# More chunks of the up stages in wide products, and a shorter lead of VectorE's subtractions, in a five-layer transformer on one core

## The chip, the core and the metric

The kernel runs on one core of one Trainium2 chip. What counts is the device time of one execution in microseconds (us), shown as the median of several runs. Engines go by their usual names: TensorE (PE in the profile; PEld is its weight load), VectorE (DVE), ScalarE (ACT), GpSimd (POOL) and SyncE (SP), which issues the weight transfers.

## What is computed

Five transformer layers on one sequence of 256 tokens and 1,024 features, all in float32: four of a first block (attention, then a gated feed-forward part), and one of a second. The feed-forward part of the first four layers is where the change lies:

```python
def conv_gated_ffn(h, w_up, conv_w, conv_b, w_down):
    u = h @ w_up
    C = u.shape[-1]
    u = lax.conv_general_dilated(u, conv_w[:, None, :].astype(u.dtype), window_strides=(1,),
                                 padding=[(CONV_W - 1, 0)], dimension_numbers=('NWC', 'WIO', 'NWC'),
                                 feature_group_count=C) + conv_b
    gate, val = jnp.split(u, 2, axis=-1)
    return (jax.nn.silu(gate) * val) @ w_down
```

`w_up` is 1,024 x 5,504 (gate and value, 2,752 features each), `w_down` 2,752 x 1,024, and the convolution takes three taps along the sequence.

## The kernel before

**Products in two parts.** A float32 matrix product is made of reduced-precision ones: every operand is kept as a high part (`w_hi`, `h_hi`) and a low part (`w_lo`, `h_lo`), and high x high, high x low and low x high are summed. `product` (line 1772 on) issues three matmuls of 256 columns for each 128 x 128 tile of weights (lines 1779 to 1781). `wide_product` (line 1785 on) issues two: the low weights with the high activations, 256 columns (line 1791), and the high weights with high and low activations side by side in `h_both`, 512 columns (line 1794). It leaves two halves in one PSUM bank, which must be added afterwards.

**Weights.** They come as 241 chunks of 1 MB. For each chunk SP issues the transfer to `w_raw` (three buffers, `RAW`), ScalarE casts it to `w_hi` (line 409), VectorE subtracts and has `w_lo` (line 953); `w_hi` and `w_lo` have five slots (`SLOTS`). SP starts the transfer of chunk c when VectorE has subtracted chunk c - 3:

```python
                if c >= RAW:
                    sp.wait_ge(lo_ready, c - RAW + 1)
```

**The up stage** has 22 chunks in a layer. Each holds 128 gate and 128 value features, which go to the banks `pj[slot]` and `val_bank[slot]`, with three slots used in turn (`RING`); chunk 21 is half of one. TensorE's first three chunks are mixed with the wait for the normalised activations (`first_outputs`, lines 1842 and 1851); then come chunks 3 to 20 one after the other, either with `outputs` (three products a tile) or `wide_outputs`, as `is_wide` says. Before each, TensorE waits for the low weights of the chunk (`lo_ready`) and for the bank to be free (`bank_free`), in `chunk_ready`.

In step j ScalarE works on chunk j in this order: for a wide chunk it copies the second halves out of the banks (line 872); it multiplies by a tap and adds the bias (line 887, twice; for a wide chunk these read the sums that VectorE makes); then it casts weight chunks up to j + `high_up(j)`, which is 4 at first and 5 from j = 3 on; then it applies the gate function (line 891). VectorE in step j: for a wide chunk it adds the halves (line 1532, twice); it adds the other taps (line 1540, four times); then it subtracts weight chunks up to j + `low_up(j)`; then, when the gate function is done, it multiplies gate and value (line 1560). GpSimd then splits the product into a high and a low part (lines 1751 and 1754). `low_up` before:

```python
            return min(AHEAD - 1, RING + j // 4)
```

that is 3 for j = 0 to 3 and 4 from j = 4 on, so step 4 subtracts two chunks.

**The down stage** follows at once. Its 11 weight chunks hold 16 tiles of 128 x 128 each in a row, 22 for each output tile. Its first product takes hidden tiles 0 to 18 of the first output tile, and waits at its start for all the weights that these need:

```python
                        n, at = divmod(f * FT + k, UNITS)
```

```python
                        pe.wait_ge(lo_ready, first + (f * FT + b - 1) // UNITS + 1)
```

With f = 0, b = 19 and `UNITS` = 16 this is the second of the down stage's weight chunks, number 23 when the up stage's are counted from 0. The second product (f = 1) needs number 24, the third output tile number 26. The last tiles (19 to 21) are taken in after both first products, when GpSimd has split the last hidden tile.

The order of work on every engine is as written: engines meet through semaphores alone.

Of the kernel before, what the change touches and what calls it, by code (L numbers as in the profile page):

```python
# [37 lines left out]
FT = 22  # L38
RING = 3
# [30 lines left out]
AHEAD = 5  # L70
HIGH = 4
RAW = 3
WIDE_UP = (range(10, 20),) * 4 + (range(2, FT),)
UNITS = STD // P
DOWN = FT * DT // UNITS

# [23 lines left out]
def build(nc, xT, w_std, params, consts, lam, onehot, tables, pT, out):  # L100
    ctx = ExitStack()
    with ctx:
# [178 lines left out]
        def is_wide(ffn, j):  # L281

            return j in WIDE_UP[ffn]

        def wide_count(ffn, j):

            return sum(len(WIDE_UP[f]) for f in range(ffn)) + j - WIDE_UP[ffn][0] + 1

# [41 lines left out]

        def low_up(j):

            return min(AHEAD - 1, RING + j // 4)

        def down_weights(c0, k):

# [604 lines left out]
        def _(dve):  # L941
# [291 lines left out]
            for kind, c0, n in STAGES:  # L1233
# [244 lines left out]
                elif kind == "up":  # L1478
                    def half_step(j, c, slot):
                        at = j * 8 + PARAM["conv"] + ffn * FT * 8  # L1480
                        dve.wait_ge(conv_init, (j + ffn * FT) * 2 + 2)
                        dve.scalar_tensor_tensor(cgate[:, slot, 1:S], pj[slot][:, 0:S - 1], par[:, at + 1:at + 2],
                                                 cgate[:, slot, 1:S], ALU.mult, ALU.add).then_inc(conv_part, 3)
                        dve.wait_ge(conv_part, (j + ffn * FT) * 3 + 3)
                        dve.scalar_tensor_tensor(cgate[:, slot, 2:S], pj[slot][:, 0:S - 2], par[:, at:at + 1],
                                                 cgate[:, slot, 2:S], ALU.mult, ALU.add).then_inc(bank_free, 1)
                        split_to(weights_of(layer, c) + low_up(j))
                        dve.wait_ge(gated, j + ffn * FT + 1)
                        dve.tensor_tensor(cval[0:HALF, slot, :], cgate[0:HALF, slot, :], cval[0:HALF, slot, :],
                                          ALU.mult).then_inc(prod_done, 1)  # L1490
# [82 lines left out]
                    for j in range(n):  # L1573
                        step(j, c0 + j, slot_of(c0, j), lambda: split_to(weights_of(layer, c0 + j) + low_up(j)))
# [999 lines left out]
```

## Time and profile before

| | us |
|---|---|
| median of 3 runs | 1479.22 |
| lowest, highest | 1477.85, 1479.90 |
| the profiled execution | 1477.22 |
| its span, first to last instruction | 1475.6 |
| TensorE busy in it | 1469.5 (100%) |
| VectorE busy | 1114.9 (76%) |
| ScalarE busy | 922.8 (63%) |
| GpSimd busy | 331.5 (22%) |
| weight load on TensorE, beside its matmuls | 1366.6 (93%) |
| DMA, mean rate | 180 GB/s |

The profile shows one execution. Busy times are sums over the span and say nothing of who waits for whom; that is read from the chain that ended last, and from the instructions of two engines laid side by side in time. Matmuls overlap in the pipeline, so the time that one costs is the distance between two starts and not the duration in its row.

### The profile page before, as it was taken

Reading aid. Unit: us, or ns where it says so; the run is one execution under the profiler, and the core shown is the slowest. Engines: PE = TensorE matmul, PEld = TensorE weight load, DVE = VectorE, ACT = ScalarE, POOL = GpSimd, SP = SyncE. Lnnn points to the kernel's source line nnn. Section 1 sums busy time; section 2 is a strip of 40 time slices with the busy share of each in tenths; the row PEclk is TensorE's granted clock in tenths of the full one; section 3 lists DMA queues with packets and bytes.
Section 4 is the critical chain, followed back from the end, with each engine's and each line's share of the span. In section 5 each row is a group of like instructions: output and inputs, shape, how many; then the busy total and the mean of one; then the engine's idle time right before and its main releaser. Section 6 shows DMA issues by size and latency. Waiting matters only on the chain.

```text
span 1475.6 us, 26859 instructions
## 1 busy us (share of the span) xinstructions
PE 1469.5 (100%) x10616; PEld 1366.6 (93%) x10616; DVE 1114.9 (76%) x1877; ACT 922.8 (63%) x1528; POOL 331.5 (22%) x461
## 2 busy tenths in 40 slices
PE   9999999999999999999999999999999999999999
PEld 8999989899999898989989899999898999988998
DVE  7778898565578995787899566688995688798645
ACT  7776666456766664575676456766764558566443
POOL 2104222211142222212222221022212361122100
PEclk9999999999999999999999999999999999999999
DMA  7644656444346555562565545445655464366450
GB/s 276 203 159 138 223 199 222 169 162 161 115 138 208 201 203 194 184 189 87 200 208 196 196 161 197 157 142 202 209 192 199 157 215 171 115 213 209 176 209 30
DMA packets 39689, 265.06 MB, mean 180 GB/s; under 512 B 5247, under 2 KB 5562, under 8 KB 8976
## 3 DMA queue, kind: packets, MB, share of 16 engines
q1 hardware_dynamic: 36432, 255.54, 49.1%
q0 software_dynamic: 2992, 7.79, 2.2%
q8 instruction: 84, 1.38, 0.4%
q14 instruction: 37, 0.30, 0.1%
q10 hardware_dynamic: 144, 0.05, 0.0%
HBM read 262.24 MB, written 1.12 MB: 178 GB/s over the span
## 4 chain that ended last, share of the span: by engine, by line
PE 98%; ACT 1%; DVE 1%; DMA 1%; issue 0%; SPq 0%; ACTq 0%
PE bank L1794 26%; PE bank L1779 15%; PE bank L1780 14%; PE bank L1781 14%; PE bank L1791 13%; PE bank L1842 6%; PE bank L1851 3%; PE bank L2025 1%; PE bank L2014 1%; PE bank L2006 1%; PE bank L2005 1%; PE bank L2379 1%; PE bank L2026 1%; DMA w_raw<-w_std 1%; PE bank L2078 0%; PE bank L2193 0%
## 5 line engine op out<-in xcount | busy, mean ns | idle before, releaser
L953 DVE TENSOR_TENSOR w_lo<-w_raw,w_hi 128x2048 fp32r<-128x2048 f32 x239 | 549.8, 2308 | 72.5 <-ACT w_hi L409 72.4
L409 ACT CAST w_hi<-w_raw 128x2048 fp32r<-128x2048 f32 x239 | 453.3, 1905 | 82.2 <-DMA w_raw<-w_std 61.9
L1794 PE MATMUL bank<-h_both,w_hi 128*128 128x512 f32 x960 | 301.5, 395 | 0.0
L1779 PE MATMUL bank<-h_both,w_hi 128*128 128x256 f32 x992 | 284.6, 287 | 0.0
L1780 PE MATMUL bank<-h_both,w_hi 128*128 128x256 f32 x992 | 280.6, 283 | 0.0
L1781 PE MATMUL bank<-h_both,w_lo 128*128 128x256 f32 x992 | 280.5, 283 | 0.0
L1791 PEld LDWEIGHTS bank<-h_both,w_lo 128*128 128x128 f32 x960 | 180.0, 188 | 42.2
L1794 PE MATMUL bank<-act_both,w_hi 128*128 128x512 f32 x672 | 212.0, 395 | 0.0
L1779 PEld LDWEIGHTS bank<-h_both,w_hi 128*128 128x128 f32 x992 | 189.9, 191 | 5.0 <-issue 4.2
L1780 PEld LDWEIGHTS bank<-h_both,w_hi 128*128 128x128 f32 x992 | 190.0, 192 | 0.3
L1781 PEld LDWEIGHTS bank<-h_both,w_lo 128*128 128x128 f32 x992 | 189.9, 191 | 0.0
L1791 PE MATMUL bank<-h_both,w_lo 128*128 128x256 f32 x960 | 188.6, 278 | 0.0
L1751 POOL CAST act_both<-tmp 128x256 f32 x110 | 53.9, 490 | 438.1 <-DVE tmp L1560 319.1
L1779 PE MATMUL bank<-act_both,w_hi 128*128 128x256 f32 x516 | 149.2, 289 | 0.0
L1791 PEld LDWEIGHTS bank<-act_both,w_lo 128*128 128x128 f32 x672 | 124.1, 188 | 26.6
L1794 PEld LDWEIGHTS bank<-h_both,w_hi 128*128 128x128 f32 x960 | 146.1, 189 | 0.0
L1780 PE MATMUL bank<-act_both,w_hi 128*128 128x256 f32 x516 | 145.9, 283 | 0.0
L1781 PE MATMUL bank<-act_both,w_lo 128*128 128x256 f32 x516 | 145.9, 283 | 0.0
L1791 PE MATMUL bank<-act_both,w_lo 128*128 128x256 f32 x672 | 135.2, 279 | 0.0
L1540 DVE SCALAR_TENSOR_TENSOR tmp<-u_sb,par,tmp 128x255 f32<-128x255 f32 x234 | 113.2, 524 | 21.7 <-ACT tmp L887 20.9
L1842 PE MATMUL bank<-h_both,w_hi 128*128 128x256 f32 x400 | 106.7, 288 | 0.3 <-DVE w_lo L1139 0.2
L1794 PEld LDWEIGHTS bank<-act_both,w_hi 128*128 128x128 f32 x672 | 103.7, 189 | 1.5
(233 smaller groups left out, 2651.1 us busy)
## 6 DMA issues: line engine op xcount, KB each, us to landing
w_raw<-w_std SPq DMA_DIRECT2D x239, 1024.0 KB, 4.9
act_both<-vec_dram POOLq DMA_DIRECT2D x56, 128.0 KB, 3.5
w_raw<-w_std SPq DMA_DIRECT2D x3, 512.0 KB, 8.3
x<-xT SPq DMA_DIRECT2D x2, 512.0 KB, 5.3
out<-x SPq DMA_DIRECT2D x3, 256.0 KB, 2.1
w_raw<-w_std SPq DMA_DIRECT2D x2, 256.0 KB, 4.8
par<-params SPq DMA_DIRECT2D x1, 446.0 KB, 6.2
cst<-consts SPq DMA_DIRECT2D x1, 256.0 KB, 9.2
```

The source lines that it names most:

```text
L409: act.copy(w_hi[:, n % SLOTS, :], w_raw[:, n % RAW, :]).then_inc(hi_ready, 1)
L953: dve.tensor_tensor(w_lo[:, n % SLOTS, :], w_raw[:, n % RAW, :], w_hi[:, n % SLOTS, :].bitcast(F32), ALU.subtract).then_inc(lo_ready, 1)
L1540: return dve.scalar_tensor_tensor(to[:, slot, lag:S], source(v)[:, 0:S - lag], par[:, bass.ds(at + (4 * v + 2 - lag), 1)], to[:, slot, lag:S],
L1751: pool.tensor_copy(act_hi[:, bass.ds(j, 1), :].squeeze(1) if not isinstance(j, int) else act_hi[rows, j, :], cval[rows, slot, :]).then_inc ...
L1779: pe.matmul(dst, wh, xh, start=first, stop=False, skip_group_check=shared)
L1780: pe.matmul(dst, wh, xl, start=False, stop=False, skip_group_check=shared)
L1781: done = pe.matmul(dst, wl, xh, start=False, stop=last, skip_group_check=shared)
L1791: pe.matmul(bank[:, 0:S], weights[k][1], moving[k][0], start=start and k == 0, stop=False, skip_group_check=True)
L1794: done = pe.matmul(bank[:, :], weights[k][0], moving[k][1], start=False, stop=stop and k == len(weights) - 1, skip_group_check=True)
L1842: pe.matmul(dst, a, b, start=k == 0 and w is wh and (n == 0 or not shared), stop=False, skip_group_check=shared)
L1851: done = pe.matmul(dst, a, b, start=False, stop=k == DT - 1, skip_group_check=shared)
L2005: pe.matmul(sc[m][:, 0:QB], q[:, 0:QB], k[:, 0:QB], start=True, stop=True)
```

## The change

Two lines. In layers 0 to 3 the up stage's wide chunks are 3 to 20 in place of 10 to 19 (`FT` is 22). And `low_up` is `RING`, 3, from chunk 14 on, in place of 4. The fifth layer's entry stays as it is, and so does `high_up`.

```diff
-WIDE_UP = (range(10, 20),) * 4 + (range(2, FT),)
+WIDE_UP = (range(3, FT - 1),) * 4 + (range(2, FT),)
...
         def low_up(j):
 
-            return min(AHEAD - 1, RING + j // 4)
+            return min(AHEAD - 1, RING + j // 4) if j < 14 else RING
```

VectorE's order in layer 0 in step 14, and so in 13 and 15, before (L1532 adds halves, L1540 taps, L953 subtracts weights, L1560 multiplies gate and value):

```order
L1532 TENSOR_TENSOR u_sb<-bank,tmp 128x256 x2
L1540 SCALAR_TENSOR_TENSOR tmp<-u_sb,par,tmp 128x255 x2
L1540 SCALAR_TENSOR_TENSOR tmp<-u_sb,par,tmp 128x254 x2
L953 TENSOR_TENSOR w_lo<-w_raw,w_hi 128x2048
L1560 TENSOR_TENSOR tmp<-tmp 128x256
```

and now, step 14 and the beginning of step 15:

```order
L1532 TENSOR_TENSOR u_sb<-bank,tmp 128x256 x2
L1540 SCALAR_TENSOR_TENSOR tmp<-u_sb,par,tmp 128x255 x2
L1540 SCALAR_TENSOR_TENSOR tmp<-u_sb,par,tmp 128x254 x2
L1560 TENSOR_TENSOR tmp<-tmp 128x256
L1532 TENSOR_TENSOR u_sb<-bank,tmp 128x256 x2
```

Step 14 has no subtraction; every later step has one, of the chunk before the one that it subtracted until now.

VectorE's order at the end of the stage, before: step 20, step 21 (L1482, L1485, L1489) and the first of the down stage (L1582, L1585):

```order
L1540 SCALAR_TENSOR_TENSOR tmp<-bank,par,tmp 128x255 x2
L1540 SCALAR_TENSOR_TENSOR tmp<-bank,par,tmp 128x254 x2
L953 TENSOR_TENSOR w_lo<-w_raw,w_hi 128x2048
L1560 TENSOR_TENSOR tmp<-tmp 128x256
L1482 SCALAR_TENSOR_TENSOR tmp<-bank,par,tmp 128x255
L1485 SCALAR_TENSOR_TENSOR tmp<-bank,par,tmp 128x254
L953 TENSOR_TENSOR w_lo<-w_raw,w_hi 128x2048
L1489 TENSOR_TENSOR tmp<-tmp 64x256
L953 TENSOR_TENSOR w_lo<-w_raw,w_hi 128x2048
L1582 TENSOR_TENSOR x<-bank,x 128x256
L1585 TENSOR_TENSOR x<-bank,x 128x256
```

and now:

```order
L1532 TENSOR_TENSOR u_sb<-bank,tmp 128x256 x2
L1540 SCALAR_TENSOR_TENSOR tmp<-u_sb,par,tmp 128x255 x2
L1540 SCALAR_TENSOR_TENSOR tmp<-u_sb,par,tmp 128x254 x2
L953 TENSOR_TENSOR w_lo<-w_raw,w_hi 128x2048
L1560 TENSOR_TENSOR tmp<-tmp 128x256
L1482 SCALAR_TENSOR_TENSOR tmp<-bank,par,tmp 128x255
L1485 SCALAR_TENSOR_TENSOR tmp<-bank,par,tmp 128x254
L953 TENSOR_TENSOR w_lo<-w_raw,w_hi 128x2048
L1489 TENSOR_TENSOR tmp<-tmp 64x256
L953 TENSOR_TENSOR w_lo<-w_raw,w_hi 128x2048 x2
L1582 TENSOR_TENSOR x<-bank,x 128x256
L1585 TENSOR_TENSOR x<-bank,x 128x256
```

Step 20 has two additions more, and its one subtraction is now of chunk 23, before of chunk 24; the one that is missing is made up behind step 21, where two stand.

## Rows read from the trace of the kernel before

**Rows 1.** The page: TensorE's busy time, and the chain that ended last by engine.

```profile
PE 1469.5 (100%) x10616; PEld 1366.6 (93%) x10616; DVE 1114.9 (76%) x1877; ACT 922.8 (63%) x1528; POOL 331.5 (22%) x461
...
PE 98%; ACT 1%; DVE 1%; DMA 1%; issue 0%; SPq 0%; ACTq 0%
```

**Rows 2.** Windows: length, busy time (instructions) by engine, clock, DMA share, GB/s.

```profile
141.59:181.90 40.31, 40.31 (x338) 40.31 (x337) 35.94 (x53) 26.93 (x34) 11.09 (x16) 1.00 0.61 219
181.91:237.60 55.69, 55.69 (x322) 48.63 (x321) 50.91 (x79) 38.21 (x59) 11.45 (x20) 1.00 0.58 199
...
743.95:799.65 55.70, 55.70 (x322) 48.64 (x321) 52.63 (x80) 39.28 (x60) 11.55 (x21) 1.00 0.59 206
```

**Rows 3.** Timeline of TensorE, from up to down stage: start, us, instruction.

```profile
246.17 0.28 PE L1781 MATMUL bank<-h_both,w_lo 128*128 128x256 f32 x1
246.29 0.40 PE L1791 MATMUL bank<-act_both,w_lo 128*128 128x256 f32 x2
...
260.24 0.28 PE L2379 MATMUL bank<-act_both,w_hi 128*128 128x256 f32 x1
```

**Rows 4.** Timeline of VectorE, one wide step; idle time before it in brackets.

```profile
204.82 0.76 DVE L1532 TENSOR_TENSOR u_sb<-bank,tmp 128x256 f32<-128x256 f32 x2 [0.17 <-ACT tmp L872]
205.92 1.76 DVE L1540 SCALAR_TENSOR_TENSOR tmp<-u_sb,par,tmp 128x255 f32<-128x255 f32 x4 [0.34 <-ACT tmp L887]
207.60 2.28 DVE L953 TENSOR_TENSOR w_lo<-w_raw,w_hi 128x2048 fp32r<-128x2048 f32 x1
209.80 0.42 DVE L1560 TENSOR_TENSOR tmp<-tmp 128x256 f32<-128x256 f32 x1
```

**Rows 5.** Timeline of VectorE, steps 2 to 5.

```profile
147.99 1.72 DVE L1540 SCALAR_TENSOR_TENSOR tmp<-bank,par,tmp 128x255 f32<-128x255 f32 x4
149.63 2.28 DVE L953 TENSOR_TENSOR w_lo<-w_raw,w_hi 128x2048 fp32r<-128x2048 f32 x1
...
152.16 1.65 DVE L1540 SCALAR_TENSOR_TENSOR tmp<-bank,par,tmp 128x255 f32<-128x255 f32 x4
...
159.11 0.43 DVE L1560 TENSOR_TENSOR tmp<-tmp 128x256 f32<-128x256 f32 x1 [3.10 <-ACT tmp L891]
...
161.21 4.49 DVE L953 TENSOR_TENSOR w_lo<-w_raw,w_hi 128x2048 fp32r<-128x2048 f32 x2
165.61 0.42 DVE L1560 TENSOR_TENSOR tmp<-tmp 128x256 f32<-128x256 f32 x1
165.94 1.65 DVE L1540 SCALAR_TENSOR_TENSOR tmp<-bank,par,tmp 128x255 f32<-128x255 f32 x4
```

**Rows 6.** Timeline of ScalarE, step 3: cast of chunk 8, then the gate function.

```profile
156.86 1.91 ACT L409 CAST w_hi<-w_raw 128x2048 fp32r<-128x2048 f32 x1 [3.62 <-DMA w_raw<-w_std]
158.66 0.42 ACT L891 ACTIVATE tmp<-tmp 128x256 f32<-128x256 f32 x1
```

**Rows 7.** DMA, 140 to 250: issues, KB each, median us to landing.

```profile
w_raw<-w_std SPq DMA_DIRECT2D x22, 1024.0 KB, 4.9
```

**Rows 8.** Timeline of VectorE, steps 19 and 21.

```profile
241.04 2.29 DVE L953 TENSOR_TENSOR w_lo<-w_raw,w_hi 128x2048 fp32r<-128x2048 f32 x1
...
252.03 0.41 DVE L1489 TENSOR_TENSOR tmp<-tmp 64x256 f32<-64x256 f32 x1
```

**Rows 9.** Timeline of VectorE, layer 2, step 4; that layer's chunk 3 starts at 703.51.

```profile
724.25 4.48 DVE L953 TENSOR_TENSOR w_lo<-w_raw,w_hi 128x2048 fp32r<-128x2048 f32 x2
```

**Rows 10.** Timeline of GpSimd, the last hidden tile of layer 0.

```profile
254.98 0.73 POOL L1754 TENSOR_TENSOR act_both<-tmp,act_both 64x256 fp32r<-64x256 f32 x1
```

**Rows 11.** Windows at the start of the program, columns as in rows 2.

```profile
1.30:5.30 4.00, 3.93 (x9) 3.19 (x10) 0.14 (x9) 1.66 (x2) 2.29 (x4) 1.00 0.76 248
5.30:7.20 1.90, 1.90 (x10) 1.52 (x8) 1.19 (x3) 1.59 (x5) 0.00 (x0) 1.00 0.96 261
```

## The prediction, written before the changed kernel ran

> I read the profile in this order: shares and chain, TensorE's counts by stretch, VectorE's order in time, then ScalarE's beside it. Times are microseconds from the start of the span, for layer 0's up stage; "chunk j" is weight chunk j of that stage (0 to 21), "step j" what VectorE or ScalarE does for it, and chunks 22 onward are the down stage's first weights.
>
> **What bounds the kernel now.** TensorE is busy 1469.5 of 1475.6 and holds 98% of the chain that ended last [rows 1]. No wait of it of even 1 stands in the up stage, so only two things can change the time: fewer or shorter matmuls, and a wait of TensorE that isn't there now. TensorE's stretch of seven three-product chunks (336 matmuls; the window counts two older ones too) takes 181.90 - 141.59 = 40.3, so 5.76 a chunk and 120 ns a matmul; the ten wide ones (320 matmuls) take 55.7, so 5.57 a chunk and 174 ns a matmul. Layer 2 shows the same [rows 2]. The down stage begins at 246.29 without a gap behind the last up matmul at 246.17 [rows 3].
>
> VectorE is the reader's second view. A wide step there is two additions, four taps, one subtraction and one product, starting at 204.82, 205.92, 207.60 and 209.80 [rows 4] (step 13); the next instruction follows a product's start by 0.33 (165.61 to 165.94) [rows 5]. That is 1.10 + 1.68 + 2.20 + 0.33 = 5.31 a step where nothing makes it wait. A three-product step is 4.1 to 4.2 (147.99 to 152.16) [rows 5]. So beside TensorE's 5.76 VectorE recovers 1.6 a chunk when late; beside wide chunks only 5.57 - 5.31 = 0.26. And it is late when the wide part would now begin: step 3 starts at 152.16, while TensorE was through with chunk 3 at 141.59 + 5.76 = 147.35.
>
> **The products: a gain of 6.1 if nothing waits.** 32 chunks (8 in each of 4 layers) times 5.76 - 5.57 = 0.19.
> The Trainium skill (TensorE: Matmul & The Clock Gate, section Back-to-back issue gap) gives the isolated gap as columns divided by 2.4 GHz plus 2.5 ns. As an estimate from that page, three products of 256 columns take 327.5 ns and one of 256 with one of 512 takes 325.0, so 32 chunks of 16 such sets would gain 1.3 and not 6.1. The rows show 360 and 348 ns here, and I go by the rows.
>
> **VectorE's and ScalarE's added work.** Each chunk that becomes wide adds two copies on ScalarE and two additions on VectorE; on VectorE the step's first tap comes 1.10 later. Step by step:
> Step 3. In the kernel before, its product waited 3.10 for ScalarE until 159.11 [rows 5]: ScalarE casts chunk 8 before the gate function of step 3, the cast began at 156.86, the gate function at 158.66 [rows 6], and chunk 8's transfer could start only when VectorE had subtracted chunk 5 (151.91, the subtraction of 149.63). This wait covers the added 1.10: product 3 stays at 159.1.
> Step 4 (two subtractions). Nothing covers it: chunk 7's subtraction starts at 162.3 in place of 161.21 and ends at 164.6; TensorE wants chunk 7 at 141.59 + 4 x 5.57 = 163.9. A wait of 0.7, new. Product 4 at 166.7.
> Steps 5 to 13, nine of them at 5.31: product 13 at 166.7 + 47.8 = 214.5. TensorE is through with chunk 13 at 203.6. VectorE is late all this time, but harmlessly: a bank is needed again only two chunks later (11.1), and the subtractions are four chunks ahead.
>
> **The lead of three from chunk 14: the term that decides.** Step 14 has no subtraction and gives 1.2 back: product 14 at 218.6 (ScalarE's cast and gate function now bound it). Product 15 at 223.9, and with it ends the subtraction of chunk 18. From here ScalarE, whose lead stays five, wants chunk j+5 in step j, whose transfer waits for the subtraction of chunk j+2, which is VectorE's in step j-1. That is the loop of step 3 again, now in every step. Its length by rows: 4.9 from issue to landing [rows 7], 0.1 until the cast, 1.80 for the cast, 0.45 for the gate function until the product (158.66 to 159.11) [rows 5, 6]. So product j can't start before the end of subtraction j+2 plus 7.25. Product 16: 223.95 + 7.25 = 231.2, not 229.2. Product 17: 236.5, which its own loop just allows (229.2 + 7.25). Product 18: 236.6 + 7.25 = 243.8. Product 19: 249.1. Step 20: additions at 249.5, taps at 250.6, subtraction of chunk 23 from 252.3 to 254.5. Two steps take 12.65, 6.3 a step, against TensorE's 5.57.
>
> **Who waits.** The first down product waits for chunk 23. Before, that subtraction was step 19's (241.04 to 243.3 [rows 8]) and TensorE came at 246.29, so 3.0 to spare. Now it is step 20's. TensorE is ready at 141.59 + 18 x 5.57 + 2.88 for the half chunk (24 matmuls of 120 ns) + 0.7 = 245.4, and waits until 254.5: **a stall of 9.1 in each of four layers**. What TensorE saved, and the 0.7, vanish in it: the down stage starts 254.5 - 246.3 = 8.3 later than before. Layer 2 gets 1.0 more, since there the double subtraction stood at 724.25, which is 20.74 into the stage and not 19.62 [rows 9], because of a later transfer. Sum 3 x 8.3 + 9.3 = 34.2.
> Behind it I cost nothing: chunk 24 (step 21) is ready about 260.7, wanted at 254.5 + 6.9; SP only follows the subtractions, already counted; POOL's last part ends 3.7 behind the half product (252.03 to 255.71 [rows 8, 10]), so about 265.9, plus ScalarE's half-tile copy of 0.4, and TensorE comes to it 13.95 after its start (246.29 to 260.24 [rows 3, 10]), at 268.5. If that cover of 2.2 goes, the excess is paid in full.
>
> **The clock.** TensorE, idle before its first matmul, starts nine of them in the first 4.0, and as many again in the next 1.9 [rows 11]: half the pace, so 1.2 GHz, for 4.0, and 2.0 lost. (The clock column reads 1.00 there; the pace says otherwise.) No row shows whether a wait of 9.1 in mid-program brings this back; TensorE's longest wait here is far shorter. Ends: 0 and 2.0 a stall. I take 1.5, nearer to the upper, since the products that follow are spaced 120 and 174 ns and not by columns alone, and lose less than half: 4 x 1.5 = 6.
> The Trainium skill (the same page, section What's actually happening) says that the throttled clock is the default and that activity releases it, which would bring the slow start back after such a wait. By that rule I keep the 6; against it the sum would be without.
>
> **Sum.** 34.2 + 6 = 40. The profiled execution took 1477.2 (1475.6 span and 1.6 around it), so 1517.4; it was 2.0 under the median of 1479.2. On the median: **1519**.
>
> **Rivals.**
> A. All as said, but the clock holds: 1479.2 + 34 = 1513. For it: no row of a fall. Chance 0.17.
> B. VectorE isn't late at step 20, so the loop costs nothing (transfers shorter than 4.9, or step 14 draining more). Then step 20's taps start 1.7 behind TensorE's end of chunk 20 (at 241.8), as step 13's do (205.92 against 181.91 + 4 x 5.57), and chunk 23 is ready at 247.5, or 248.2 with the wait for chunk 7: 1.2 to 1.9 later than 246.3 in each layer, 1484 to 1487. Against it: 0.26 a step drains too little, and the loop's 3.10 is seen. Chance 0.07.
> C. Faster. If chunk 23 were subtracted before TensorE ends chunk 21, at 244.7, only the gain of 6.1 would be left: 1473. The point that decides is that one subtraction: it must end 9.8 sooner than I reckon, and even a VectorE that is never late misses it by 3. Chance 0.03, for an error in my count of chunks.
> D. The change has no effect, since the new branch meets work that has slack. The order of VectorE's instructions shows the additions and the missing subtraction, so 0.02, at 1479.
>
> **How the numbers follow.** Forecast 0.71, 1519. Its own spread: the loop turns three times per layer, and transfers 0.5 longer each time add 6 in all; a clock cost of 0 to 2.0 a stall is 1513 to 1521; a VectorE lateness that drains 1 more takes 4 off. Range 1506 to 1529, which holds A and leaves out B to D and about a tenth of the forecast. A difference of 0.2% (3) is what a measurement of this kernel can tell. Faster 0.03, within 0.2% 0.02, slower 0.95.
>
> **What would show it.** In the trace after: matmuls of the up stage at 174 ns; one idle of TensorE of 8 to 10 ahead of each of the four first down products, released by VectorE's subtraction; ScalarE's cast waiting 3 for its transfer in steps 16, 18 and 20, and VectorE's product for the gate function; VectorE's share up by 32 x 0.76 = 24; matmuls behind the stall at about half pace. Wrong if TensorE's idle at those four places is under 5, or if it sits elsewhere.

## The result, and the profile after

| | before | after |
|---|---|---|
| median, us | 1478.53 (4 runs) | 1536.97 (4 runs) |
| lowest, highest | 1477.69, 1479.90 | 1535.68, 1537.66 |
| span of the profiled execution | 1475.6 | 1535.0 |
| mean granted clock of TensorE | 1.000 | 0.985 |

The ratio is 1.0388, with a 95% interval of 1.0376 to 1.04: the change costs 58 us. The forecast was 40 more, and the range ended at 1529. The sign and the place were right, the size was a third short.

The page of the kernel after: TensorE and the others by busy time, the granted clock in 40 slices, the chain that ended last, and three groups.

```profile
PE 1478.0 (96%) x10104; PEld 1346.1 (88%) x10104; DVE 1152.2 (75%) x1941; ACT 940.5 (61%) x1592; POOL 341.2 (22%) x461
...
PEclk9999998999999989999999999999998999999999
...
PE 64%; DVE 16%; issue 8%; DMA 6%; ACT 5%; POOL 1%; SPq 0%; ACTq 0%; POOLq 0%
...
L409 ACT CAST w_hi<-w_raw 128x2048 fp32r<-128x2048 f32 x239 | 452.9, 1904 | 122.6 <-DMA w_raw<-w_std 102.2
...
L1791 PE MATMUL bank<-act_both,w_lo 128*128 128x256 f32 x672 | 139.2, 285 | 37.0 <-issue 36.8
L1779 PE MATMUL bank<-act_both,w_hi 128*128 128x256 f32 x516 | 150.0, 291 | 2.3 <-issue 2.3
```

TensorE held 98% of the chain before [rows 1] and holds 64% now; VectorE, the DMA queues and ScalarE hold 27% together. The clock dips in three of the slices. The down stage's products (L1791 with `act_both`) stand still for 37.0 where they had stood for 0: that is the stall of the forecast, 9.2 a layer. And the fifth layer's down products (L1779), of which the prediction says nothing, have an idle of 2.3.

TensorE of the kernel after, its order in time: the last up product and the first down product of layer 0, the first down product of layers 1 to 3, and that of the fifth layer.

```profile
248.17 0.28 PE L1781 MATMUL bank<-h_both,w_lo 128*128 128x256 f32 x1
258.04 0.77 PE L1791 MATMUL bank<-act_both,w_lo 128*128 128x256 f32 x2 [9.60 <-issue]
...
570.39 0.55 PE L1791 MATMUL bank<-act_both,w_lo 128*128 128x256 f32 x1 [9.67 <-issue]
...
847.38 0.55 PE L1791 MATMUL bank<-act_both,w_lo 128*128 128x256 f32 x1 [8.01 <-issue]
...
1157.43 0.55 PE L1791 MATMUL bank<-act_both,w_lo 128*128 128x256 f32 x1 [9.50 <-issue]
...
1436.66 0.35 PE L1779 MATMUL bank<-act_both,w_hi 128*128 128x256 f32 x1 [2.25 <-issue]
```

"issue" is the profile's word for a wait that it can't assign. VectorE's row settles it: its subtraction of chunk 23 starts at 255.66 and takes 2.28, so it ends at 257.94, and TensorE starts 0.10 later. VectorE of the kernel after, steps 19 and 20:

```profile
252.39 0.43 DVE L1560 TENSOR_TENSOR tmp<-tmp 128x256 f32<-128x256 f32 x1
252.73 0.75 DVE L1532 TENSOR_TENSOR u_sb<-bank,tmp 128x256 f32<-128x256 f32 x2
253.82 1.92 DVE L1540 SCALAR_TENSOR_TENSOR tmp<-u_sb,par,tmp 128x255 f32<-128x255 f32 x4 [0.34 <-ACT tmp L887]
255.66 2.28 DVE L953 TENSOR_TENSOR w_lo<-w_raw,w_hi 128x2048 fp32r<-128x2048 f32 x1
```

What follows the stall is slower too. Windows of the kernel after, columns as in rows 2: the stall, the 80 matmuls that start behind it, the same cut where the clock changes, and the fifth layer's start.

```profile
248.30:258.00 9.70, 0.15 (x2) 0.00 (x0) 9.26 (x13) 4.96 (x8) 1.50 (x3) 0.76 0.43 154
258.00:274.40 16.40, 16.36 (x80) 14.25 (x81) 8.74 (x7) 6.32 (x8) 6.45 (x4) 0.83 0.67 236
258.00:263.50 5.50, 5.46 (x17) 4.71 (x18) 3.88 (x4) 2.39 (x4) 1.13 (x2) 0.50 0.55 191
263.60:274.40 10.80, 10.80 (x64) 9.44 (x64) 4.82 (x3) 3.83 (x5) 5.32 (x2) 1.00 0.74 261
1436.60:1441.20 4.60, 4.54 (x25) 4.57 (x26) 3.90 (x6) 1.43 (x4) 1.13 (x2) 0.63 0.67 228
```

Behind the stall 17 matmuls start in 5.50 at a granted clock of 0.50, the 1.2 GHz level, and the next 64 in 10.80 at 1.00. From the start of the first to the start of the last, these 80 took 13.71 before (246.29 to 260.00); now they take 16.34, 15.85, 15.74 and 15.57 in the four layers, 8.6 more together.

**Where the 59.4 of span went.** From chunk 3's first product to the first down product a layer took 104.70 before (141.59 to 246.29, and within 0.13 of it in the other three layers); now 115.82, 115.23, 116.79 and 117.26. That is 11.1, 10.5, 12.0 and 12.6, or 46.2. The slow clock adds the 8.6, the fifth layer 4.0 (its wait of 2.4, and 1.6 of slow clock behind it), the program's start 0.6.

### The profile page after: what moved, and what is told of

Its sections match the earlier page's. It is cut to its first block, busy times and chain, and to the rows that moved or that the text cites. A ratio compares the mean times of both kernels' runs of the same rounds, so it can differ in the third digit from the quotient of the medians.

```text
span 1535.0 us, 25963 instructions
## 1 busy us (share of the span) xinstructions
PE 1478.0 (96%) x10104; PEld 1346.1 (88%) x10104; DVE 1152.2 (75%) x1941; ACT 940.5 (61%) x1592; POOL 341.2 (22%) x461
## 3 DMA queue, kind: packets, MB, share of 16 engines
HBM read 262.24 MB, written 1.12 MB: 172 GB/s over the span
## 4 chain that ended last, share of the span: by engine, by line
PE 64%; DVE 16%; issue 8%; DMA 6%; ACT 5%; POOL 1%; SPq 0%; ACTq 0%; POOLq 0%
PE bank L1794 14%; PE bank L1779 10%; PE bank L1780 9%; PE bank L1781 9%; DVE tmp L1540 8%; PE bank L1791 7%; DMA w_raw<-w_std 6%; PE bank L1842 5%; DVE w_lo L953 4%; PE bank L1851 2%; ACT tmp L887 2%; DVE tmp L1560 2%; DVE u_sb L1532 1%; PE bank L2025 1%; ACT w_hi L409 1%
## 5 line engine op out<-in xcount | busy, mean ns | idle before, releaser
L953 DVE TENSOR_TENSOR w_lo<-w_raw,w_hi 128x2048 fp32r<-128x2048 f32 x239 | 548.5, 2304 | 72.5 <-ACT w_hi L409 72.3
L1794 PE MATMUL bank<-h_both,w_hi 128*128 128x512 f32 x1472 | 463.5, 396 | 0.0
L1791 PEld LDWEIGHTS bank<-h_both,w_lo 128*128 128x128 f32 x1472 | 276.3, 188 | 79.2 <-DVE w_lo L953 14.7
L1791 PE MATMUL bank<-h_both,w_lo 128*128 128x256 f32 x1472 | 290.8, 279 | 10.8 <-DVE w_lo L953 10.8
L1794 PEld LDWEIGHTS bank<-h_both,w_hi 128*128 128x128 f32 x1472 | 224.7, 189 | 0.0
L1794 PE MATMUL bank<-act_both,w_hi 128*128 128x512 f32 x672 | 217.0, 403 | 0.0
L1540 DVE SCALAR_TENSOR_TENSOR tmp<-u_sb,par,tmp 128x255 f32<-128x255 f32 (+1 forms) x362 | 182.5, 555 | 32.5 <-ACT tmp L887 31.8
L1791 PEld LDWEIGHTS bank<-act_both,w_lo 128*128 128x128 f32 x672 | 127.9, 194 | 66.0 <-issue 37.5
L1791 PE MATMUL bank<-act_both,w_lo 128*128 128x256 f32 x672 | 139.2, 285 | 37.0 <-issue 36.8
L1751 POOL CAST act_both<-tmp 128x256 f32 x110 | 62.5, 568 | 500.1 <-DVE tmp L1560 365.0
L887 ACT ACTIVATE tmp<-u_sb,par 128x256 f32<-128x256 f32 x181 | 100.3, 596 | 116.4 <-DVE u_sb L1532 108.9
L1779 PE MATMUL bank<-act_both,w_hi 128*128 128x256 f32 x516 | 150.0, 291 | 2.3 <-issue 2.3
L1779 PE MATMUL bank<-h_both,w_hi 128*128 128x256 f32 x480 | 139.6, 291 | 0.0
L1780 PE MATMUL bank<-h_both,w_hi 128*128 128x256 f32 x480 | 135.7, 283 | 0.0
L1781 PE MATMUL bank<-h_both,w_lo 128*128 128x256 f32 x480 | 135.6, 283 | 0.0
L1794 PEld LDWEIGHTS bank<-act_both,w_hi 128*128 128x128 f32 x672 | 106.8, 194 | 1.5
L1842 PE MATMUL bank<-h_both,w_hi 128*128 128x256 f32 x400 | 106.7, 288 | 1.3 <-DVE w_lo L1139 1.2
L1842 PE MATMUL bank<-h_both,w_lo 128*128 128x256 f32 x400 | 104.5, 283 | 0.0
L1779 PEld LDWEIGHTS bank<-act_both,w_hi 128*128 128x128 f32 x516 | 99.4, 193 | 5.6 <-issue 5.4
```

Of the source, the lines that this page charges most:

```text
L887: act.activation(to[:, slot, :], source, ACT.Identity, bias=col(3), scale=col(2)).then_inc(conv_init, 1)
L953: dve.tensor_tensor(w_lo[:, n % SLOTS, :], w_raw[:, n % RAW, :], w_hi[:, n % SLOTS, :].bitcast(F32), ALU.subtract).then_inc(lo_ready, 1)
L1540: return dve.scalar_tensor_tensor(to[:, slot, lag:S], source(v)[:, 0:S - lag], par[:, bass.ds(at + (4 * v + 2 - lag), 1)], to[:, slot, lag:S],
L1751: pool.tensor_copy(act_hi[:, bass.ds(j, 1), :].squeeze(1) if not isinstance(j, int) else act_hi[rows, j, :], cval[rows, slot, :]).then_inc ...
L1779: pe.matmul(dst, wh, xh, start=first, stop=False, skip_group_check=shared)
L1780: pe.matmul(dst, wh, xl, start=False, stop=False, skip_group_check=shared)
```

## The experiments

The change has two parts, so the first question was which costs what. The first four kernels share a comparison: the kernel before took 1479.96 in it.

**The shorter lead alone.**

```diff
-WIDE_UP = (range(3, FT - 1),) * 4 + (range(2, FT),)
+WIDE_UP = (range(10, 20),) * 4 + (range(2, FT),)
```

> Only the shorter lead from chunk 14; the wide chunks are 10 to 19 as before. Theory (the loop of subtraction, transfer, cast, gate function and product, 12.7 us for two steps, opens as soon as VectorE leads by three while ScalarE leads by five): VectorE is on time at step 14 and still falls behind, chunk 23 is ready near 250.9 and TensorE is there at 246.2, a stall of 4.6 in each of layers 0 to 3 (18.5 together), no clock fall or a short one, and the 4.0 of the fifth layer: 1501 us. Rival (the loop only bites a VectorE that is already late): chunk 23 comes one step later but on time, at 247.5, 1.2 a layer: 1484 to 1488 us.

Measured: 1511.26 (1510.96 to 1513.41), ratio 1.0215 (1.0198 to 1.0232). TensorE of this kernel, layer 0's first down product:

```profile
251.40 0.77 PE L1791 MATMUL bank<-act_both,w_lo 128*128 128x256 f32 x2 [4.73 <-issue]
```

The stall is the one that the loop gives, and ScalarE's casts wait for transfers for 137.1 in all where they waited 61.9 before. So the shorter lead makes TensorE stop even where VectorE has no more to do than before. The 10 over the expectation are the clock: it fell at each of these stalls, and the part that takes 13.7 before took 16.4, 16.2, 15.7 and 16.4. The fifth layer waited 2.51, its clock stayed at 1.00, and it cost 2.7 and not the 4.0 expected.

**The wide products alone.**

```diff
-            return min(AHEAD - 1, RING + j // 4) if j < 14 else RING
+            return min(AHEAD - 1, RING + j // 4)
```

> Only the wide chunks 3 to 20; the lead stays four. Theory (a late VectorE recovers 0.1 a wide step, since its step is 5.48 and not 5.31 when late): chunk 23 is subtracted in step 19, ready near 249.4 where TensorE comes at 245.6; the down stage starts 3.2 later than before in each of layers 0 to 3, fifth layer unchanged, no clock fall: 1478.5 + 13 = 1491 us. Rival (all of the loss is the lead's): the gain of the products shows, 1472.5 us.

Measured: 1498.42 (1496.65 to 1499.36), ratio 1.0119 (1.0102 to 1.0136). TensorE of this kernel, then its window behind the stall.

```profile
252.12 0.77 PE L1791 MATMUL bank<-act_both,w_lo 128*128 128x256 f32 x2 [3.77 <-issue]
```

```profile
252.10:268.50 16.40, 16.38 (x80) 14.25 (x81) 11.53 (x14) 8.07 (x10) 5.41 (x6) 0.84 0.72 257
```

With the lead of four the loop is gone (ScalarE's casts wait 28.5 for transfers in the whole program), and a stall of 3.8 stays. The down stage of layer 0 starts 3.3 later than before, where the expectation had 3.2 with its step of 5.48; what the expectation missed is the clock, which fell here too and cost 7.3 in the four layers. The program also began 2.5 later in this execution, in part by a stretch at 0.50 near its start.

Neither part is harmless alone, and 31 and 18 fall short of 58. What adds up is VectorE's lateness: counted from chunk 3's first product, the subtraction of chunk 23 in layer 0 ended at 101.7 before, 7.7 later with the lead alone, 6.2 later with the wide chunks alone and 14.0 later with both. What doesn't add up is the slack of 3.0 that stood between this subtraction and TensorE: each part alone has it to use up, and both together have it only once. In four layers that is 12, and it makes the 21.0 and 12.4 that the two parts add to the up stages into nearly the 46.2 of both. Each stall also pays for the clock, 1.5 to 2.7, whether it is 3.5 long or 9.7.

**ScalarE's lead shortened as well**, in the changed kernel:

```diff
-            return min(AHEAD, RING + 1 + j // 3)
+            return min(AHEAD, RING + 1 + j // 3) if j < 14 or j == FT - 1 else RING + 1
```

> The changed kernel, with ScalarE's casts one chunk less ahead too in steps 14 to 20 (four in place of five), so that each cast's transfer waits for a subtraction two steps old. Theory (loop): no wait for a transfer in steps 15 to 20, steps of 5.5, chunk 23 ready near 253.4 and not 257.2: 3.9 less in each of four layers, stalls of about 7.8 with a clock fall behind them, and nothing lost in the fifth layer: 1537 - 15.5 - 4 = 1517 us. Rival (the transfers' latency isn't what holds steps 15 to 20): 1533 to 1537 us.

Measured: 1517.31 (1514.4 to 1521.14), ratio 1.0259 (1.024 to 1.0279). The stall in layer 0 is 7.08. VectorE of this kernel, the products of three steps in a row:

```profile
238.90 0.41 DVE L1560 TENSOR_TENSOR tmp<-tmp 128x256 f32<-128x256 f32 x1
...
244.40 0.41 DVE L1560 TENSOR_TENSOR tmp<-tmp 128x256 f32<-128x256 f32 x1
...
249.89 0.41 DVE L1560 TENSOR_TENSOR tmp<-tmp 128x256 f32<-128x256 f32 x1
```

But for the 0.34 that the first tap of every wide step waits for ScalarE, no wait stands in these steps, and each takes 5.50, where the kernel after has 6.3. The loop was the whole of that difference: ScalarE five ahead beside VectorE three ahead, with three raw buffers between them. It also showed that in this kernel a late wide step takes 5.5, and not the 5.31 of my sum.

**The fifth layer with its old lead**, in the changed kernel:

```diff
-            return min(AHEAD - 1, RING + j // 4) if j < 14 else RING
+            return min(AHEAD - 1, RING + j // 4) if j < 14 or layer == 4 else RING
```

> The changed kernel, but the fifth layer keeps its lead of four. Theory: the fifth layer's stall of 2.4 and the slow clock behind it go, 4.0 less: 1533 us. Rival (that layer's 4.0 come from the stages ahead): 1537 us.

Measured: 1534.47 (1532.97 to 1537.23), ratio 1.0363, against 1.0388 for the changed kernel in its own comparison. TensorE of this kernel reaches its last down stage without a gap:

```profile
1438.27 0.62 PE L1794 MATMUL bank<-h_both,w_hi 128*128 128x512 f32 x2
1438.74 0.28 PE L1779 MATMUL bank<-act_both,w_hi 128*128 128x256 f32 x1
```

The gap and the slow clock behind it are gone, and this layer's up stage takes 111.5 again, as before the change. The time fell by less than the spread of the runs, so the 4.0 are read from the trace and not from the times.

**Why a late step takes 5.5.** VectorE of the kernel after, one step of layer 0, then GpSimd of the same kernel:

```profile
184.26 0.41 DVE L1560 TENSOR_TENSOR tmp<-tmp 128x256 f32<-128x256 f32 x1
184.60 0.74 DVE L1532 TENSOR_TENSOR u_sb<-bank,tmp 128x256 f32<-128x256 f32 x2
185.68 1.94 DVE L1540 SCALAR_TENSOR_TENSOR tmp<-u_sb,par,tmp 128x255 f32<-128x255 f32 x4 [0.34 <-ACT tmp L887]
187.54 2.28 DVE L953 TENSOR_TENSOR w_lo<-w_raw,w_hi 128x2048 fp32r<-128x2048 f32 x1
189.74 0.42 DVE L1560 TENSOR_TENSOR tmp<-tmp 128x256 f32<-128x256 f32 x1
```

```profile
184.84 0.40 POOL L1751 CAST act_both<-tmp 128x256 f32 x1 [4.17 <-DVE tmp L1560]
185.41 0.73 POOL L1754 TENSOR_TENSOR act_both<-tmp,act_both 128x256 f32 x1 [0.18 <-POOL act_both L1751]
```

Product to product is 189.74 - 184.26 = 5.48, and the part that grew is the taps: 187.54 - 185.68 = 1.86, where my row gave 1.68 [rows 4]. In rows 4 the additions had waited for ScalarE's copy, and by the time the taps came GpSimd was all but through with its subtraction. A VectorE that is late doesn't wait for the copy. Its taps come 1.42 behind its product instead of 1.69, and fall on GpSimd's subtraction (185.41 to 186.14). By form, the first taps of the kernel before at 188 to 238, then of the kernel after at 153 to 245:

```profile
L1540 DVE SCALAR_TENSOR_TENSOR tmp<-u_sb,par,tmp 128x255 f32<-128x255 f32 x18 | 8.8, 492 | 3.1 <-ACT tmp L887 3.1
```

```profile
L1540 DVE SCALAR_TENSOR_TENSOR tmp<-u_sb,par,tmp 128x255 f32<-128x255 f32 x32 | 18.5, 616 | 5.4 <-ACT tmp L887 5.4
L1540 DVE SCALAR_TENSOR_TENSOR tmp<-u_sb,par,tmp 128x254 f32<-128x254 f32 x32 | 13.8, 471 | 0.0
```

Half of the 128x255 taps are the first of their step; the mean of both halves went from 492 to 616, so the first went up by about 250 (0.50 to 0.755 in single steps), while the 128x254 ones, which come after GpSimd is done, keep 471. In all 18 wide steps of layer 0 (3 to 20) the first tap ends 0.28 behind the end of GpSimd's subtraction.

The Trainium skill (SBUF — State Buffer, section Who interferes with whom) says that a VectorE instruction with two inputs in SBUF contends with a GpSimd instruction that reads SBUF, and that the one issued first blocks the other. The rows agree: both inputs of these taps (`u_sb`, `tmp`) are in SBUF, GpSimd's subtraction starts first, and the tap takes 0.25 more. The kernel before already has the effect in step 1 of layer 0, and in step 20 it has taps that read their bank in PSUM. GpSimd's subtraction and VectorE's taps in these two steps:

```profile
143.29 2.70 POOL L1754 TENSOR_TENSOR act_both<-tmp,act_both 128x256 f32 x1 [0.19 <-POOL act_both L1751]
145.30 2.15 DVE L1540 SCALAR_TENSOR_TENSOR tmp<-u_sb,par,tmp 128x255 f32<-128x255 f32 x4
...
244.21 1.72 DVE L1540 SCALAR_TENSOR_TENSOR tmp<-bank,par,tmp 128x255 f32<-128x255 f32 x4 [0.55 <-ACT tmp L887]
244.40 0.75 POOL L1754 TENSOR_TENSOR act_both<-tmp,act_both 128x256 f32 x1 [0.18 <-POOL act_both L1751]
```

The first four taps read `u_sb` and take 2.15, the first of them 0.97, and it too ends 0.28 behind the subtraction (145.99). The other four read the bank, and neither they (1.72, as in rows 5; the second starts inside the subtraction and takes 0.48) nor the subtraction (0.75) is longer. So a row of the kernel before could have told it.

Two kernels were to test this: the wide products alone, with GpSimd's subtractions moved out of the way, and a control with the same rewriting of GpSimd's loop (from a loop with register addresses to one written out) and nothing moved. These, and the two after them, share a comparison in which the kernel before took 1479.45.

```diff
-                    with pool.Fori(0, n // RING) as i:
-                        for k in range(RING):
-                            split_act(i * RING + k, i * RING + (c0 + k), slot_of(c0, k))
-                    for j in range(n // RING * RING, n):
-                        split_act(j, c0 + j, slot_of(c0, j))
+                    def held(j):
+                        return ffn < 4 and 3 <= j < 16
+
+                    for j in range(n):
+                        split_act(j, c0 + j, slot_of(c0, j), 0)
+                        if held(j - 1):
+                            split_act(j - 1, c0 + j - 1, slot_of(c0, j - 1), 2)
+                        split_act(j, c0 + j, slot_of(c0, j), 1)
+                        if not held(j):
+                            split_act(j, c0 + j, slot_of(c0, j), 2)
```

Part 0 is the wait for VectorE's product, 1 the cast, 2 the subtraction. The control differs in one line:

```diff
-                        return ffn < 4 and 3 <= j < 16
+                        return False
```

> Only the wide chunks (lead four), and in steps 3 to 15 of layers 0 to 3 GpSimd's subtraction (0.74 us) runs one step later, ahead of the next cast, so that it lies beside VectorE's two additions and not beside its first tap; its loop is written out. Theory (the first tap of a late VectorE takes 0.76 and not 0.50 us because GpSimd's subtraction runs at that moment): the first tap is back at 0.5, a step takes 5.3 to 5.35 us and not 5.48, thirteen steps gain 1.9 to 2.5, and the stall of 3.7 before the down stage falls to 1.2 to 1.8; with little or no slow clock behind it 1498.4 - 4 x 2.2 - up to 6 = 1484 to 1490 us. Rival (the first tap is long for another reason, ScalarE's write of the same tile or the wait itself): 1498 us.

> Only the wide chunks (lead four), with GpSimd's loop written out and nothing moved: the control for the run before. Both theories: 1498 us, as with the loop.

Measured: 1482.29 (1481.46 to 1485.09) with the subtractions held back, ratio 1.0024 (1.0015 to 1.0034), and **1480.20** (1479.45 to 1483.46) for the control, ratio 1.001 (1.0001 to 1.0019). The first came a little below the 1484 to 1490 expected, its 128x255 taps (steps 4 to 16) back at a mean of 484. The control was to stay at 1498 and didn't: writing the loop out was enough. GpSimd of the wide-only kernel, then of the control, in the same step:

```profile
154.97 0.40 POOL L1751 CAST act_both<-tmp 128x256 f32 x1 [2.94 <-DVE tmp L1560]
155.55 0.74 POOL L1754 TENSOR_TENSOR act_both<-tmp,act_both 128x256 f32 x1 [0.18 <-POOL act_both L1751]
```

```profile
153.60 0.40 POOL L1754 CAST act_both<-tmp 128x256 fp32r<-128x256 f32 x1 [3.04 <-DVE tmp L1560]
154.08 0.74 POOL L1757 TENSOR_TENSOR act_both<-tmp,act_both 128x256 fp32r<-128x256 f32 x1
```

In the wide-only kernel VectorE's product ended at 154.8, its taps began at 155.81 and GpSimd's subtraction ran until 156.29. In the control the product ended at 153.54, the taps began at 154.54 and the subtraction ran until 154.82: 0.5 into the taps there, 0.3 here. GpSimd begins its cast 0.06 behind the product in place of 0.17, and its subtraction 0.1 sooner behind the cast. Those 0.2 save most of what the tap lost (mean 521, against 617 in the wide-only kernel at 153 to 245), and a late wide step of the control takes 5.31, the very number of my sum. Some 16 late steps by 0.17 are 2.7 a layer, the stall of 3.8 shrinks to 0.95, the clock doesn't fall, and 18 are gone.

```profile
247.96 0.47 PE L1799 MATMUL bank<-act_both,w_lo 128*128 128x256 f32 x2 [0.95 <-issue]
```

So the theory of the tap holds, and it is the length of the overlap that counts, which I had not foreseen: with none the first tap took 0.48, with 0.22 (rows 4) 0.50, with 0.28 (the control) 0.56, with 0.48 (the kernel after) 0.76. The other reasons that the expectation named are out, since ScalarE writes the same tile, and the tap waits the same 0.34 for it, in all of these. The kernel in which I moved the work was no better than the control that moved nothing: where the holding ends, GpSimd has two subtractions in a row, and that step takes 5.70 in place of 5.31; in layer 0 the product of step 5 also waited 0.96 for ScalarE, whose cast waited for a transfer.

**TensorE kept busy in the stall**, in the changed kernel: 18 matmuls whose result nothing uses, ahead of the first down product of layers 0 to 3.

```diff
+                    if layer < 4:
+                        for _ in range(18):
+                            pe.matmul(ov[:, 0:S], rstd[:, 0:P], rstd[:, :], start=True, stop=True)
```

> The changed kernel, with 18 more matmuls of TensorE (256 columns, result unused) ahead of the first down product in layers 0 to 3, where it would wait: 18 x 0.43 = 7.7 us of a stall of 8.2 to 9.8. Theory (an idle TensorE comes back at half pace, which costs 1.9 to 2.6 a layer): granted clock 1.0 throughout layers 0 to 3, the first down products take 13.7 and not 15.6 to 16.3 us, 1537 - 8.7 = 1528 us. Rival (those products are slow because their data or weights are late): 1537 us.

Measured: 1532.23 (1529.66 to 1534.85), ratio 1.0361 (1.0346 to 1.0376). The granted clock was 1.00 throughout. Window behind the stall, and TensorE of this kernel at the end of it:

```profile
259.55:275.50 15.95, 14.17 (x80) 12.21 (x81) 8.75 (x7) 6.38 (x8) 6.45 (x4) 1.00 0.59 206
```

```profile
274.81 0.51 PE L1791 MATMUL bank<-act_both,w_lo 128*128 128x256 f32 x2 [1.75 <-ACT act_both L904]
```

Neither theory's time came, but the clock held. The matmuls went at full pace again, and then TensorE waited for the last hidden tile: 1.9, 0.6, 0.8 and 1.8 in the four layers, 5.1 of the 8.7 gained. In the changed kernel the slow clock hid this wait. From the first down product to the first matmul of L2379 the four layers took 16.6, 16.1, 16.0 and 15.8 there and take 16.0, 14.8, 14.9 and 16.0 here, so what the slow clock behind the stalls costs the changed kernel in the end is about 3, and not 8.6. The profiled execution is shorter by 5.3, but 2.6 of this lie in the fifth layer, which the edit doesn't touch: its wait was 1.14 and its clock stayed at 1.00.

The last hidden tile is late for a reason of the change itself. VectorE and GpSimd behind the half product, in the kernel before, then in the kernel after:

```profile
252.37 2.27 DVE L953 TENSOR_TENSOR w_lo<-w_raw,w_hi 128x2048 fp32r<-128x2048 f32 x1
252.50 2.40 POOL L1751 CAST act_both<-tmp 64x256 fp32r<-64x256 f32 x1 [2.54 <-DVE tmp L1489]
```

```profile
266.15 4.48 DVE L953 TENSOR_TENSOR w_lo<-w_raw,w_hi 128x2048 fp32r<-128x2048 f32 x2
266.29 4.59 POOL L1751 CAST act_both<-tmp 64x256 fp32r<-64x256 f32 x1 [4.90 <-DVE tmp L1489]
```

GpSimd's cast, which takes 0.40 where VectorE isn't at a subtraction (184.84 above), starts 0.13 behind the first subtraction and ends about 0.26 after the last, and two subtractions now stand where one stood. That is the contention of the tap with the engines exchanged, and it takes 2.2.

**Fewer wide chunks, the old lead.** If VectorE's lateness is what costs, then the range that starts where it can still drain should cost nothing. `WIDE_UP` with `range(8, FT - 1)`, lead of four:

> The lead stays four and the wide chunks are 8 to 20: five chunks at 5.76 ahead of them, in which VectorE recovers 1.6 each. Theory: chunk 23 is ready 0.5 before TensorE wants it, no stall, and the three additional wide chunks gain 3 x 0.19 x 4 = 2.3: 1477.5 us, just under the kernel before (1479.9 in the last comparison). Rival (VectorE is later than reckoned by over 0.5): a stall of up to 1 a layer, 1478 to 1482 us.

Measured: 1476.70 (1475.58 to 1482.19), ratio 0.9985 (0.9974 to 0.9996). No gap of even 0.1 ahead of the down stages; chunk 23 was ready 0.9, 0.7, 0.1 and 0.5 before TensorE came.

The last three kernels share a comparison in which the kernel before took 1478.75. First `range(7, FT - 1)`, lead of four, GpSimd's loop written out:

> Lead four, wide chunks 7 to 20, GpSimd's loop in the up stages written out. Theory: its cast and subtraction start 0.2 us earlier, a late VectorE's step is 5.32 to 5.37 and not 5.48, so it recovers enough from chunk 7 on; chunk 23 is ready 0.6 ahead of TensorE, no stall, four wide chunks more in each of four layers: 4 x 4 x 0.19 = 3.1 less than before, 1476.4 against 1479.5. Rival (the late VectorE still misses it): 1478 to 1481.

Measured: 1475.37 (1474.61 to 1479.53), ratio 0.998 (0.9971 to 0.9989), span 1473.5. Then `range(6, FT - 1)`, with the first down products' wait split, so that they can start with what is there:

```diff
-                        down(f, 0, early)
+                        down(0, 0, UNITS)
...
+                        down(0, UNITS, early)
+                        down(1, 0, 2 * UNITS - FT)
+                        down(1, 2 * UNITS - FT, early)
```

> Lead four, wide chunks 6 to 20, GpSimd's loop written out, and in layers 0 to 3 the first down product waits for chunk 22 alone, for chunk 23 only ahead of its tile 16, and the second product for chunk 24 only ahead of its tile 10. Theory: the stall hangs on that one wait, so TensorE starts the down stage at once; the next limit, GpSimd's last hidden tile, is just met: 5 chunks x 4 x 0.19 = 3.8 less, 1475.6. Rival (the last hidden tile becomes the wait): 1476 to 1479.

Measured: 1476.20 (1474.58 to 1477.43), ratio 0.9978 (0.9969 to 0.9988), span 1473.0: the same as the one before it. One more wide chunk is worth 0.8, which the times can't tell. The split was hardly used: in three layers chunk 23 was ready 0.1 to 0.4 before TensorE came to the down stage, and only in the fourth 0.5 after. Last, the kernel before with nothing but GpSimd's loop written out:

> The kernel before with nothing but GpSimd's loop in the up stages written out. Theory (an earlier GpSimd helps only a late VectorE; here VectorE waits for TensorE in the wide steps): no difference, 1479 to 1480. Rival (the loop itself costs time): 1476 or less.

Measured: 1478.58 (1478.01 to 1479.8), ratio 1.0001 (0.9991 to 1.001). Where VectorE isn't late, GpSimd's 0.2 are worth nothing; the gain of the two kernels above is that of the products.

## Why the prediction came out as it did

- **The products, 6.1.** Right. The 32 wide chunks more are 512 matmuls fewer in the page (10616 to 10104). From chunk 3's first product to the first down product layer 0 took 104.69 before, 104.13 with three wide chunks more, 103.95 with four and 103.76 with five, so 0.19 a chunk, the forecast's price. (The spans of the first two shrank by 1.5 and 2.1, where the price gives 2.3 and 3.0, in part because their chunk 3 began 0.4 and 0.5 later.) The estimate of 1.3 for all 32 was too small.
- **The wait for chunk 7, 0.7.** Right in place, 0.53 in layer 0. The kernel after has a second such wait, for chunk 20, of 1.46, 1.12, 2.65 and 3.18 in the four layers, that the sum lacked. Both come out of time that TensorE would have waited at the stall.
- **The loop of 12.65 per two steps.** Right: step 16's product stands at 234.10, step 18's at 246.77, step 20's at 259.49, so 12.67 and 12.72, and ScalarE's casts wait 3.27, 3.01 and 2.96 in just the steps named. The loop's ends were as the rows gave them. Removing it removed the wait.
- **"Steps 5 to 13, nine of them at 5.31": the step that failed.** It is 5.48. The number was put together from two states that don't occur together in this kernel: the 0.33 behind a product came from steps in which VectorE was late [rows 5], the taps' 1.68 from a step in which it was not [rows 4]. A late step meets more of GpSimd's subtraction. With 5.48 VectorE recovers 0.09 a chunk beside wide products instead of 0.26. Followed through layer 0, with the program's later start of 0.6 taken off: step 16's product was to stand at 231.2 and stands at 233.5, 2.3 later. Ten late steps (5 to 13 and 15) by 0.17 are 1.7 of it, and 0.5 is a wait of step 5's product for ScalarE. From there the loop keeps its length; step 18 to 19 takes 5.62 in place of 5.31, step 20's tap adds 0.2, and chunk 23 is ready 2.8 late, at 257.3 where the sum had 254.5. VectorE's busy time says the same: it was to rise by 24 and rose by 37.3, and 72 wide steps by 0.17 are 12.
- **The other layers.** Over the forecast the four layers are 2.8, 2.2, 2.7 and 4.3 late, 12.0 together, and about 8 of this is the tap, 0.17 in twelve steps of each. Step 16 took 7.40 and 7.19 in the first two layers but 8.69 and 9.21 in the last two, where ScalarE's cast waited 4.56 and 5.08 for its transfer in place of 3.27 and 3.06; the runs don't show why these transfers took longer. The 1.0 that layer 2 was to have more for its late double subtraction didn't come: its step 15 stands within 0.2 of layer 1's. It is longer than layers 0 and 1 by the slow transfer alone. The 3.4 at 0.50 in its up stage delayed TensorE and not chunk 23, and are no part of the 2.7.
- **The stall.** Its place was right in all four layers, with 9.75, 9.83, 8.17 and 9.66 against the 9.1 named. It is close to the forecast only because TensorE, held up inside the stage by 2.2 to 5.5, came later too, and that is luck. Who had read the stall alone would have called the sum right.
- **The clock.** "I take 1.5" a stall: 2.15 were measured (2.6, 2.1, 2.0 and 1.9), just above the upper end of 2.0. Rival A, the clock that holds, is out: it fell to 0.50 at all four stalls. Behind the waits of about 1 in the control it did not fall.
- **The cover of 2.2 behind the stall.** Named, and left at nothing. GpSimd's 3.7 behind the half product was read beside one subtraction of VectorE's, and the change puts two there, which by itself takes the 2.2 (GpSimd and ScalarE are through 6.3 behind the half product and not 4.1). That nothing of it was seen is luck: the slow clock hid it. With the clock held it was paid, as the prediction's last clause on it says.
- **The fifth layer: put at nothing without a reason, the second step that failed.** `low_up` is read by all five layers; the front of the text says that the fifth layer's entry stays, which is so for `WIDE_UP` alone. It cost 4.0.
- **Rivals B to D** are out: VectorE is late, and a stall of over 5 stands at all four places.

So 34.2 became 46.2, 6 became 8.6, and 4.0 and 0.6 were missed. That is 59.4 against 40.2. The kernel with the lead alone, whose stalls are half as long, pays as much for the clock as the one with both, because only the part of the slow stretch that lies behind the restart costs anything. In layer 0 of the kernel after the clock stood at 0.50 from 253.4 to 263.6, 4.7 of it inside the stall and 5.6 behind it; with the lead alone from 250.4 to 257.2, 1.0 inside and 5.8 behind. In the other layers 3.3 to 3.9 and 4.0 to 5.7 lie behind it.

## What to carry to other kernels

Before a lead is shortened, find the one piece of work for which the next stage's first instruction waits, and count in which step it will stand; a stage that is bound by TensorE throughout can still be stopped by it. And take an engine's step time from steps in the state that the change will bring: an engine that is late starts its instructions at other moments, beside other work of its neighbours, and may be slower for that. Where two engines take turns on few buffers, leads that lie too far apart, here five and three with three raw buffers, make a loop of transfer, cast and subtraction that runs in every step. And ask of every function that the diff touches who else reads it.

## What the runs showed of the hardware

- VectorE's tap with both inputs in SBUF took 0.755 in place of 0.50 when it began inside a GpSimd subtraction that also reads SBUF, and ended 0.28 behind it. Taps of the same kind behind it kept 0.47, and one with an input in PSUM kept 0.48 beside such a subtraction. The other way round, GpSimd's cast (0.40 by itself) took 2.40 beside one subtraction of VectorE's and 4.59 beside two in a row, and ended about 0.26 behind them.
- GpSimd's loop with register addresses began its cast 0.17 behind the product that it waited for, and the written-out one 0.06; between cast and subtraction it was 0.18 and 0.08. Worth nothing in the kernel before, and 18 us in one that lived on that margin.
- TensorE's clock fell to the 1.2 GHz level at every wait of 3.5 or more ahead of a down stage (3.51 to 9.67). At shorter ones no length decides: it fell at 2.25 (the kernel after, fifth layer), 2.47 (the kernel with the fifth layer's old lead, layer 3) and 2.65 (the kernel after, layer 2), and held at 2.4 GHz at 2.18 (the kernel with the subtractions held back, layer 0), 2.51 (the lead alone, fifth layer) and 3.18 (the kernel after, layer 3). Some 15 us into the program it fell behind waits of under 0.8 in two kernels (the wide products alone, and the kernel before with the loop written out). One fall cost 1.5 to 2.7 us; an idle of 4 cost nearly as much as one of 9.6.
